# Two fused layers on one Trainium2 core: wide projections with the activations stationary, turned back by TensorE

## The reference

```
# layer 1
h = rms_norm(x, norm1_w); proj = h @ w_in            # 2048 -> 5648: q k v z xbc dt
attn = causal softmax attention (8 heads of 128, q and k normalised per head)
ssm  = Mamba-2 scan over silu(conv4(xbc)), gated by silu(z), normalised
x = x + concat(attn, ssm) @ w_out
h = rms_norm(x, norm2_w)
u = causal_dwconv(h @ w_up, ffn_conv_w, ffn_conv_b)  # 2048 -> 11264, 3 taps over positions
u_gate, u_val = split(u, 2)
x = x + (silu(u_gate) * u_val) @ w_down              # 5632 -> 2048
# layer 2
mod = silu(c) @ w_ada + b_ada; shift, scale, gate = split(mod, 3)
h = rms_norm(x, gain) * (1 + scale) + shift
proj = h @ w_in_2                                    # 2048 -> 7168
y = concat(dilated attention * silu(z_a), retention * silu(z_r))
out = rms_norm(x + gate * (y @ w_out_2), final_gain)
```

## Time and profile before

| | us |
|---|---|
| three runs, median (lowest to highest) | 1661.17 (1660.32 to 1661.61) |
| the profiled execution | 1661.47 |
| its span, first to last instruction | 1659.8 |
| TensorE busy in it | 1607.7 (97%) |
| VectorE busy | 1160.1 (70%) |
| ScalarE busy | 807.0 (49%) |

### The profile page before, as it was taken

One profiled execution on the slowest core, in us unless ns is written; L12 is line 12 of the kernel. 1 busy time (PEld: TensorE's weight loads), 2 busy tenths in 40 slices (PEclk: granted clock), 3 DMA queues, 4 the chain that ended last, 5 costly groups with the idle time before them and its releaser, 6 DMA issues.

```text
span 1659.8 us, 33703 instructions
## 1 busy us (share of the span) xinstructions
PE 1607.7 (97%) x13254; PEld 1577.9 (95%) x13254; DVE 1160.1 (70%) x1357; ACT 807.0 (49%) x972; POOL 26.2 (2%) x53
## 2 busy tenths in 40 slices
PE   6999999999999999999999999999799999999997
PEld 6998899989999999999999999999799999999996
DVE  5776678675668888888888888576664544664755
ACT  6444345544554545545455454444455544444542
POOL 0000000000000000000000000000000000000000
PEclk9999999999999999999999999999999999999998
DMA  8454344455548777787787876555455555455451
GB/s 326 130 176 140 127 148 142 144 197 176 186 153 331 262 281 291 252 299 260 269 293 257 303 265 210 184 189 189 152 178 187 184 189 166 139 165 168 163 178 52
DMA packets 85043, 336.17 MB, mean 203 GB/s; under 512 B 9440, under 2 KB 9696, under 8 KB 78560
## 3 DMA queue, kind: packets, MB, share of 16 engines
q1 hardware_dynamic: 77328, 281.34, 49.6%
q0 software_dynamic: 7056, 51.38, 8.4%
q10 hardware_dynamic: 576, 2.24, 0.4%
HBM read 332.82 MB, written 2.10 MB: 202 GB/s over the span
## 4 chain that ended last, share of the span: by engine, by line
PE 72%; DVE 5%; issue 2%; ACT 1%; DVEq 0%; ACTq 0%
PE PS L1086 23%; PE PS L1088 23%; PE PS L1090 23%; DVE ada_w L921 1%; DVE wlo L577 1%; ACT whi L253 1%; PE PS L1188 1%; DVE UV L879 1%; PE PS L1155 1%; PE PS L1332 0%; DVE X L1073 0%; PE PS L1174 0%; DVE X L593 0%; DVE rb L611 0%; PE PS L1133 0%
## 5 line engine op out<-in xcount | busy, mean ns | idle before, releaser
L1086 PE MATMUL PS<-gh,whi 128*128 128x256 f32 x3520 | 999.5, 284 | 20.2 <-DVE wlo L577 15.1
L1088 PE MATMUL PS<-gl,whi 128*128 128x256 f32 x3520 | 985.7, 280 | 0.0
L1090 PE MATMUL PS<-gh,wlo 128*128 128x256 f32 x3520 | 984.0, 280 | 0.0
L577 DVE TENSOR_TENSOR wlo<-raw,whi 128x1024 fp32r<-128x1024 f32 x528 | 644.9, 1224 | 430.7 <-ACT whi L253 429.4
L253 ACT ACTIVATE whi<-raw 128x1024 fp32r<-128x1024 f32 x528 | 557.2, 1058 | 728.8 <-PE PS L1090 727.5
L1086 PEld LDWEIGHTS PS<-gh,whi 128*128 128x128 f32 x3520 | 664.6, 189 | 27.9 <-issue 24.7
L1088 PEld LDWEIGHTS PS<-gl,whi 128*128 128x128 f32 x3520 | 664.1, 189 | 2.8 <-issue 1.9
L1090 PEld LDWEIGHTS PS<-gh,wlo 128*128 128x128 f32 x3520 | 663.1, 188 | 0.0
L1086 PE MATMUL PS<-ah,whi 128*128 128x256 f32 x704 | 197.2, 280 | 11.0 <-DVE UV L879 7.3
L1088 PE MATMUL PS<-al,whi 128*128 128x256 f32 x704 | 195.8, 278 | 0.0
L1090 PE MATMUL PS<-ah,wlo 128*128 128x256 f32 x704 | 195.7, 278 | 0.0
(11 more groups left out here) (186 smaller groups left out, 803.1 us busy)
## 6 DMA issues: line engine op xcount, KB each, us to landing
raw<-weights SPq DMA_DIRECT2D x528, 512.0 KB, 3.4
ada_w<-w_ada POOLq DMA_DIRECT2D x48, 1024.0 KB, 5.3
X<-xT SPq DMA_DIRECT2D x4, 512.0 KB, 11.9
outT<-X SPq DMA_DIRECT2D x4, 512.0 KB, 2.6
c<-const ACTq DMA_DIRECT2D x1, 1536.0 KB, 6.4
c_act<-c_rows POOLq DMA_DIRECT2D x1, 1024.0 KB, 9.3
prm<-params SPq DMA_DIRECT2D x1, 276.5 KB, 3.8
mask<-const ACTq DMA_DIRECT2D x1, 256.0 KB, 9.4
```

Of the source, the lines that this page charges most:

```text
L577: dve.tensor_tensor(wlo[:, j % SPLIT, :], raw[:, j, :], whi[:, j % SPLIT, :].bitcast(F32), ALU.subtract).then_inc(s_lo, 1)
L1086: pe.matmul(out[:, t, :], whi[:, b, w], hi[:, kt, :], start=first and half == 0 and t % 2 == 0, stop=False, skip_group_check=True)
L1088: pe.matmul(out[:, t, :], whi[:, b, w], lo[:, kt, :], start=False, stop=False, skip_group_check=True)
L1090: mm = pe.matmul(out[:, t, :], wlo[:, b, w], hi[:, kt, :], start=False, stop=last and half == 1, skip_group_check=True)
```

## The change

In the 376 units of the two input projections and of the up projection the operands change places. `product_natural` holds a 128 x 128 piece of the activations (one input tile, 128 positions) stationary and streams the unit's 512 weight columns: two input tiles, two halves of the positions, three matmuls, 12 in all. The group's result has positions on the partitions. It must be turned back, in three steps: ScalarE copies the two PSUM banks to SBUF (`natural`, `ffn_natural`), TensorE transposes eight 128 x 128 blocks into PSUM (`turn`), one unit later, and then the group is landed.

In the input projections the copy goes to the group's final place, the transposes into the same two banks, and VectorE (layer 1) or ScalarE (layer 2, `landed2`) lands them, one slot later than before. The steps that follow in layer 1 (convolution, silu) move back a slot. In the feed-forward the copy goes to a new buffer `UN`, multiplied by the norm's factor, which is now one number per partition (`r2`, from `sum_columns`); it frees the banks at once. The transposes go to PSUM banks 4 to 7, and the convolution reads them there. The reductions are spread: 3 in layer 1's output stage, 5 in the first feed-forward pair, then 4 in each iteration. The output and down projections keep `product`.

The diff, cut to its core:

```diff
@@ -71,7 +71,8 @@
-ADA_STEP = 6
+ADA_STEP = 4
+ADA_FIRST = ADA_TILES - ADA_STEP * (FF_GROUPS - 1)
...
-        UG, o = place("UG", [P, 4, S + 2], offset=area)
-        UV, o = place("UV", [P, 4, S + 2], offset=o)
+        UN, o = place("UN", [P, 2, 4, S], offset=area)
...
+        def landing1(g):
+
+            return U[:, 4 * g:4 * g + 4, 3:3 + S] if g < 3 else QKVZ[:, 4 * (g - 3):4 * (g - 3) + 4, :]
+
+        def ffn_turned(val):
+
+            return acc_tiles(3 if val else 2)
+
+        r2 = small[:, 224:226]
...
@@ ScalarE @@
+            def natural(k, last, par, dst):
+
+                act.wait_ge(s_used, last + 1 + SPLIT)
+                act.activation(dst, acc_tiles(par), ACT.Copy).then_inc(s_nat, 1)
...
             for n in range(IN_SLOTS):
+                if n % 8 == 7:
+                    natural(n // 8, 8 * B_IN + n, (G_IN + n // 8) % 2, landing1(n // 8))
                 split(B_IN, LEAD + n)
                 slot1(n)
...
+            def ffn_natural(val, last, grp, par):
+
+                act.wait_ge(s_used, last + 1 + SPLIT)
+                act.wait_ge(s_evac, grp + 2)
+                for c in range(2):
+                    ins = act.activation(UN[:, val, 2 * c:2 * c + 2, :], acc_tiles(par)[:, 2 * c:2 * c + 2, :], ACT.Copy,
+                                         scale=r2[:, c:c + 1])
+                    ins.then_inc(s_unat, 1)
+                act.sem_inc(s_evac, 1)
...
             for n in range(IN2_SLOTS):
-                split(B_IN2, LEAD + n)
                 if n % 8 == 7:
                     g = n // 8
-                    act.wait_ge(s_used, 8 * B_IN2 + n + 1 + SPLIT)
-                    act.activation(QB[:, 4 * g:4 * g + 4, :], acc_tiles((G_IN2 + g) % 2), ACT.Copy).then_inc(s_evac, 1)
+                    natural(11 + g, 8 * B_IN2 + n, (G_IN2 + g) % 2, QB[:, 4 * g:4 * g + 4, :])
+                split(B_IN2, LEAD + n)
+                if n % 8 == 0 and n:
+                    landed2(n // 8 - 1)
                 slot2(n)
...
@@ VectorE @@
             def land(g):
 
-                finished(8 * (B_IN + g) + 7, G_IN + g)
-                dve.tensor_tensor(QKVZ[:, 4 * (g - 3):4 * (g - 3) + 4, :], acc_tiles((G_IN + g) % 2),
+                dve.wait_ge(s_turn, g + 1)
+                if g == 0:
+                    dve.wait_ge(s_rb, 1)
+                dve.tensor_tensor(landing1(g), acc_tiles((G_IN + g) % 2),
                                   rb[:, :].unsqueeze(1).to_broadcast([P, 4, S]), ALU.mult).then_inc(s_evac, 1)
...
-            def ffn_evac(last, grp, par, dst):
-                finished(last, grp)
-                dve.tensor_tensor(dst[:, :, 2:2 + S], acc_tiles(par), rb[:, :].unsqueeze(1).to_broadcast([P, 4, S]),
-                                  ALU.mult).then_inc(s_evac, 1)
...
-                dve.scalar_tensor_tensor(dst[:, t, :], src[:, t, 1:1 + S], prm[:, bass.ds(k + 2, 1)], dst[:, t, :],
+                dve.scalar_tensor_tensor(dst[:, t, 1:S], u[:, t, 0:S - 1], prm[:, bass.ds(k + 2, 1)], dst[:, t, 1:S],
...
@@ TensorE @@
+            def product_natural(b, par, tiles, first, last):
+
+
+                for half in range(2):
+                    kt = tiles[half]
+                    w = slice(512 * half, 512 * half + 512)
+                    for c in range(2):
+                        rows = slice(P * c, P * c + P)
+                        out = PS[:, 2 * par + c, :]
+                        pe.matmul(out, gh[:, kt, rows], whi[:, b, w], start=first and half == 0, stop=False)
+                        pe.matmul(out, gh[:, kt, rows], wlo[:, b, w], start=False, stop=False)
+                        mm = pe.matmul(out, gl[:, kt, rows], whi[:, b, w], start=False, stop=last and half == 1)
+                mm.then_inc(s_used, 1)
+
+            def turn(src, dst, signal):
+
+
+                for c in range(2):
+                    for t in range(4):
+                        mm = pe.transpose(dst[:, t, P * c:P * c + P],
+                                          src[:, 2 * c + t // 2, P * (t % 2):P * (t % 2) + P], ident)
+                mm.then_inc(signal, 1)
...
+            def ffn_turn(i, val):
+                pe.wait_ge(s_unat, i * 4 + (4 if val else 2))
+                if i is not first:
+                    pe.wait_ge(s_ftap, i * 16 + (0 if val else -8))
+                turn(UN[:, val, :, :], ffn_turned(val), s_uturn)
...
             for n in range(IN_SLOTS):
                 stream_in(B_IN, G_IN, n, lambda kt: kt + 1)
+                if n % 8 == 0 and n:
+                    turned_back(n // 8 - 1, (G_IN + n // 8 - 1) % 2, landing1(n // 8 - 1))
                 slot1(n)
...
             with pe.Fori(1, FF_GROUPS) as i:
                 whole(i * 3 + (B_FF - 1), i * 6 + (G_FF - 4), G_FF % 2, need_ff)
-                whole(i * 3 + B_FF, i * 6 + (G_FF - 3), (G_FF + 1) % 2, need_ff)
-                down(i - 1, i * 24 + 8 * (B_FF + 1), i * 6 + (G_FF - 2))
+                whole(i * 3 + B_FF, i * 6 + (G_FF - 3), (G_FF + 1) % 2, need_ff, i)
+                down(i - 1, i * 24 + 8 * (B_FF + 1), i * 6 + (G_FF - 2), ah, al, i)
```

More of the change, by code:

```diff
@@ L452, in ffn_hi @@
                 act.activation(hi[:, :, :], CG[:, :, :], ACT.Copy).then_inc(s_ah, 1)
[L454 to L459, removed]
+            for j in range(8):
+                if j == 7:
+                    root_columns()
+                    act.wait_ge(s_rb, 2)
+                    ffn_natural(0, 8 * B_FF + 7, G_FF, G_FF % 2)
+                split(B_FF, LEAD + j)
+            for j in range(8):
+                if j == 7:
+                    ffn_natural(1, 8 * B_FF + 15, G_FF + 1, (G_FF + 1) % 2)
                 split(B_FF + 1, LEAD + j)
-            act.wait_ge(s_evac, G_FF + 2 + 2)
+                if j == 1:
+                    ffn_base(0, False)
             ffn_base(0, True)
@@ L954, in ffn @@
                         ffn_product(i)
-            dve.wait_ge(s_c, 1)
-            with dve.Fori(1, 1 + ADA_TILES // ADA_STEP) as i:
-                ffn(i, True)
-            for i in range(1 + ADA_TILES // ADA_STEP, FF_GROUPS):
+            with dve.Fori(1, last) as i:
                 ffn(i)
+            ffn(last)
             dve.wait_ge(s_ada, ADA_TILES)
@@ L1106, in stream_in, with whole @@
+            def whole(blk, grp, par, need, after_first=None):
+                pe.wait_ge(s_evac, grp + 1)
+                for u in range(8):
+                    pe.wait_ge(s_lo, blk * 8 + (u + 1))
+                    pe.wait_ge(s_gl, need(2 * u + 1))
+                    product_natural(u % SPLIT, par, (2 * u, 2 * u + 1), u == 0, u == 7)
+                    if u == 0 and after_first is not None:
+                        ffn_turn(after_first, 0)
             def stream_in(blk, grp, n, need):
@@ L1133, in sum_squares, with sum_columns @@
                     mm = pe.matmul(PS[:, 4, 0:S], ones, buf[:, 1, t, :], start=False, stop=(t == 3))
+                mm.then_inc(s_ss, 1)
+            def sum_columns(buf):
+                pe.wait_ge(s_sum, 4)
+                pe.wait_ge(s_root, 1)
+                for t in range(8):
+                    if t >= 4:
+                        pe.wait_ge(s_sq, 7 + t)
+                    for c in range(2):
+                        mm = pe.matmul(PS[:, 4 + c, 0:1], buf[:, t // 4, t % 4, P * c:P * c + P], ones[:, 0:1],
+                                       start=(t == 0), stop=(t == 7))
                 mm.then_inc(s_ss, 1)
```

166 lines of the change are left out of this document (98 added, 68 removed).

## The result

The changed kernel is slower: 1698.18 us, median of 4 runs (1697.65 to 1698.37), against 1660.74 for the kernel before (1660.25 to 1661.61, 4 runs). The ratio is 1.0224, with a 95% interval of 1.0208 to 1.0240. The forecast was 1616 us. The profiled execution took 1698.12 us, span 1696.5.

The account below looks back on a forecast made before the run. TensorE was taken as the bound, its 256-column matmuls limited by weight loads. Terms -82.2 + 41.0 - 8.6 + 1.5 + 3.0 = -45.3 us, from 1661.2 to 1616 us; forecast 1605 to 1628, range 1600 to 1650.

Parts of the forecast that it names:

- TensorE bounds the kernel: Whole kernel: TensorE busy 97% of the span, so time is its number of instructions times their spacing.
- So I take the matmuls of before to be bound by weight loads: 256-column matmuls: a weight load of about 112 ns outlasts the 107 ns stream, with a few ns of jostling on top.
- the 216 ns of the sum: Halved matmuls in 376 units: 512 columns start 216 ns apart, a unit takes 2.59 us, together -82.2 us.
- The row of four fp32 loads with nothing to stream: Trace row of four 128x128 fp32 loads with 16-column matmuls, read as a weight load alone needing about 112 ns.
- The rows that were to prove it: Plain fp32 rows (216 ns) and lower-clock fp32r rows (0.21 to 0.22 us), read as showing no 11 ns excess.
- rival 2: Excess belongs to the fp32r stream: a 512-column matmul takes up to 235 ns, 1702 us or less; chance 0.08.
- The turns: 47 groups, 8 fp32 transposes each on TensorE at 0.109 us: +41.0 us.
- Do the turns wait: Turns' waits for ScalarE's copy are hidden, except the first feed-forward pair's second turn before the loop: +1.5 us, once.
- The wait that goes: Feed-forward iterations: TensorE's 1.07 us wait for VectorE's landing in UV goes eight times, -8.6 us.
- they might fall into the 113 ns level: The other, unswapped matmuls drop to 113 ns, up to 13 us, giving a time below 1605; chance 0.03.
- The head norms: Where VectorE's head-norm reciprocals set the pace, a faster TensorE gains nothing: +3.0 us given back, bounds 0 and 6.
- The unit of the feed-forward stage: Feed-forward unit of 24 matmuls taken as 2.80 us without waits, 2.59 after the change: 36.6 us off over 176 units.

Follow-up runs that it names:

- experiment 3: The changed kernel with two of the eight transposes of each turn, the other six blocks not turned: 1668.56 us, 29.6 less than the changed kernel, single run.
- experiment 12: A kernel of its own, TensorE alone: both operand orders at offsets 0 to 240 bytes after different forerunners; narrow 113.5 to 120.0 ns, wide 226.7 to 234.3.
- experiment 4: A kernel of its own, TensorE alone: both programs' matmul orders with buffer addresses varied; narrow 119.8 ns at 0 and 113.3 at 192 bytes, wide 227.6 and 229.1.

## Why the prediction was wrong, point by point

- **TensorE bounds the kernel**: right, before and after.
- **"So I take the matmuls of before to be bound by weight loads"**: this step failed, and with it the 216 ns of the sum. The measured term is -6.6 us in place of -82.2. The excess over 106.7 ns goes with the fp32r columns, 6.6 ns per 256 at least (113.3 less 106.7), and the rest of it, up to 7 ns, with addresses and with what ran before. The row of four fp32 loads with nothing to stream had a number, 112 ns, near enough to 117 to look like the cause. Two numbers that agree are no cause: what was needed was a row in which load and stream differ, and the trace had none of type fp32r at full clock.
- **The rows that were to prove it** The earlier trace rows are of another kind. A record of plain fp32 spends 215.8 ns on 256 columns, and at the lower granted clock fp32r spends 213 ns on them: in both a column takes 0.83 ns or more, twice the 0.44 of fp32r at full clock, and the excess does not show. The prediction itself named this against the fp32 rows, under rival 2, and gave it 0.08. **Rival 2 came true**, at 233 to 234 ns of its "up to 235", and 1698 of its 1702 us (as close as that by luck: its matmuls had 10 us too much, and it had not the 9 us of the down projection). What spoke for it was in the same trace: two levels for the same work, which one fixed load time does not explain.
- **The turns**: right. 47 x 0.880 = 41.4 us in the trace against 41.0, and 105 ns a transpose by experiment 3 against 109; the about 275 ns of the Trainium skill ("TensorE: Matmul & The Clock Gate", Part 4: PE-mode transpose) is their length, 272 here, and not their price.
- **Do the turns wait**: right. 1.4 us before the loop, against 1.5, and nothing elsewhere.
- **The wait that goes**: right that it goes, all eight, with its 8.6 us. But they are given back: the matmuls with ah/al became slower by 6 to 9 us in the kernels that lack the wait at 64 bytes (the changed one 250.8 us, the two runs of spread reductions 248.7 and 247.9, against 241.8), and the sum had no such term. The forecast's only remark on these matmuls, that they might fall into the 113 ns level, had the wrong sign.
- **The head norms**: the 3.0 us did not show as such. With a wide matmul as slow as two narrow ones, TensorE is no faster there and has nothing to give back. All that the ledger does not name came to -0.2 us.
- **The unit of the feed-forward stage**: its 2.80 us are an average over up and down units. By itself an up unit took 24 x 117.8 = 2.83 us and a down unit 2.75.

The forecast's sum with the measured terms: 1616 + 75.6 (matmuls) + 0.4 (turns) + 9.0 (down projection) - 3.2 (head norms and all else) = 1698 us.

**What is not settled.** The 17 cycles for 16 columns are read from spacings alone; what takes the time was not seen, only that it is gone at the lower clock. Which level the kernel enters at a given place, and why spreading the reductions moves it, was not predicted by any of the runs: experiment 12 shows that a forerunner can switch it, experiment 4 that addresses matter, and that the level of the down projection is switched in this way is only argued. Nor is it known why a short load frees the narrow matmul and not the wide one.

## What to carry to other kernels

Before an instruction is made half as frequent and twice as long, find out whether its excess is paid per instruction or per column, with a row of the same data type in which the two differ; a row of another type, even with the same stream time and the same load, does not answer it. If no such row is in the trace, the range has to hold both answers, and the extra work that the change needs (here 41 us of turns) is then the forecast's sure part. A row at the lower granted clock does not answer it either: here it hid the excess. A buffer's offset that was tuned for one shape of matmul has to be tuned again for another, and moving any buffer ahead of it undoes the tuning.

## What the runs showed of the hardware

- fp32r matmuls, each with its own load, start 113.3 ns apart at 256 columns and 226.7 at 512 at best, as if 16 columns took 17 cycles. bf16 has 109.1 and 216.0.
- At the lower granted clock fp32r shows 213 and 427 ns, the columns at 1.2 GHz and no more.
- A plain fp32 matmul stands in the trace as two records, 215.8 ns each at 256 columns.
- The spacing of fp32r matmuls hangs on the addresses of both operands: at 256 columns it lies up to 6.7 ns over its lowest level, at 512 up to 7.6. For 256 columns an offset of 0 is among the worst (119.8) and for 512 nearly the best (227.3); 64 bytes is better than 0 for 256 columns (117.8 or 113.3) and worse for 512 (233.4).
- The same instructions at the same addresses run at 113.3 or at 117.8 ns, by what ran before them.
- Plain fp32 transposes of 128x128 start 109 ns apart in the middle of fp32r matmuls, though each is 272 ns long, and eight of them lengthen the stream by 0.88 us.
